# The third feed-forward group by seven products, with its token sums and its gate's weight sums on GpSimd

## The reference, cut to what matters

```
def swiglu(hn, w_ffn_in, w_ffn_out):      # hn 512 x 1024, after an RMS norm with gain
    a, b = jnp.split(hn @ w_ffn_in, 2, axis=-1)
    return (jax.nn.silu(a) * b) @ w_ffn_out        # inner width 2816
```

## Time and profile before

| | us |
|---|---|
| median of 3 runs (1831.33 to 1831.77) | 1831.52 |
| the profiled execution, its own time | 1831.15 |
| its span | 1829.3 |
| mean granted TensorE clock | 0.997 of full speed |

### The profile page before, as it was taken

How to read it: one execution, slowest core, us unless ns; L and a number is a source line. 1 busy time by engine, 2 the same in 40 slices (tenths; PEclk the granted TensorE clock), 3 DMA queues, 4 the chain that set the end, 5 groups by cost and what they waited for, 6 DMA issues and landing times.

```text
span 1829.3 us, 27260 instructions
## 1 busy us (share of the span) xinstructions
PE 1799.5 (98%) x10778; PEld 1594.2 (87%) x10778; DVE 1281.3 (70%) x1741; ACT 812.4 (44%) x1027; POOL 179.3 (10%) x97
## 2 busy tenths in 40 slices
PE   9999999999999999999999999999999999999996
PEld 8898989887888878788888999998898888999995
DVE  7566665753654737446587878887898786888786
ACT  5666666533223323224453343344545752343342
POOL 2000000010000000000001234230000001224310
PEclk9999999999999999999999999999999999999998
DMA  5012111132222221222512322322476412232331
GB/s 187 26 67 70 46 46 47 47 127 81 70 86 86 83 89 46 92 70 92 183 51 92 116 92 92 115 93 95 113 185 179 144 70 93 97 111 92 103 105 46
DMA packets 25986, 170.25 MB, mean 93 GB/s; under 512 B 2736, under 2 KB 5040, under 8 KB 6320
## 3 DMA queue, kind: packets, MB, share of 16 engines
q1 hardware_dynamic: 24176, 156.51, 24.5%
q0 software_dynamic: 1728, 12.58, 3.3%
HBM read 154.40 MB, written 2.10 MB: 86 GB/s over the span
## 4 chain that ended last, share of the span: by engine, by line
PE 90%; DVE 5%; ACT 2%; issue 2%; DMA 0%; POOL 0%; DVEq 0%; SPq 0%; ACTq 0%
PE psum L705 28%; PE psum L707 28%; PE psum L706 28%; DVE normed L1992 1%; PE psum L907 1%; PE psum L902 1%; PE psum L1049 1%; DVE h L2082 1%; ACT w_hi L1334 1%; PE psum L856 0%; ACT X_hi L1334 0%; PE psum L928 0%; PE psum L1255 0%; DMA h<-in_xfm 0%; ACT std L1334 0%
## 5 line engine op out<-in xcount | busy, mean ns | idle before, releaser
L705 PE MATMUL psum<-X_hi,w_hi 128*128 128x512 f32 (+2 forms) x1392 | 463.7, 333 | 2.8 <-issue 1.2
L707 PE MATMUL psum<-X_hi,w_lo 128*128 128x512 f32 (+2 forms) x1392 | 457.3, 329 | 0.0
L706 PE MATMUL psum<-X_lo,w_hi 128*128 128x512 f32 (+2 forms) x1392 | 457.2, 328 | 0.0
L1975 DVE TENSOR_TENSOR w_lo<-w_raw,w_hi 128x2048 fp32r<-128x2048 f32 x121 | 278.5, 2303 | 93.8 <-ACT w_hi L1334 93.4
L1334 ACT ACTIVATE w_hi<-w_raw 128x2048 fp32r<-128x2048 f32 x133 | 253.6, 1907 | 186.7 <-PE psum L707 149.6
L705 PEld LDWEIGHTS psum<-X_hi,w_hi 128*128 128x128 f32 x1392 | 262.6, 189 | 30.6 <-issue 5.9
L706 PEld LDWEIGHTS psum<-X_lo,w_hi 128*128 128x128 f32 x1392 | 263.0, 189 | 25.9 <-issue 2.4
L707 PEld LDWEIGHTS psum<-X_hi,w_lo 128*128 128x128 f32 x1392 | 262.5, 189 | 23.5
L705 PE MATMUL psum<-M_hi,w_hi 128*128 128x512 f32 x320 | 124.6, 389 | 0.0
L706 PE MATMUL psum<-M_lo,w_hi 128*128 128x512 f32 x320 | 124.6, 389 | 0.0
L707 PE MATMUL psum<-M_hi,w_lo 128*128 128x512 f32 x320 | 124.5, 389 | 0.0
(11 more groups left out here) (364 smaller groups left out, 3989.8 us busy)
## 6 DMA issues: line engine op xcount, KB each, us to landing
w_raw<-in_units SPq DMA_DIRECT2D x140, 1024.0 KB, 4.9
w_lo<-w_raw POOLq DMA_DIRECT2D x12, 1024.0 KB, 6.9
h<-in_xfm SPq DMA_DIRECT2D x4, 528.0 KB, 5.6
h<-in_xfm SPq DMA_DIRECT2D x1, 2112.0 KB, 9.3
decay<-in_dec SPq DMA_DIRECT2D x4, 512.0 KB, 5.6
out<-h SPq DMA_DIRECT2D x4, 264.0 KB, 2.3
out<-h SPq DMA_DIRECT2D x2, 496.0 KB, 2.9
rot<-in_consts SPq DMA_DIRECT2D x1, 528.0 KB, 6.9
```

Of the source, the lines that this page charges most:

```text
L705: nc.tensor.matmul(dst, w2[0], x2[0], start=first, stop=False, skip_group_check=True)
L706: nc.tensor.matmul(dst, w2[0], x2[1], start=False, stop=False, skip_group_check=True)
L707: m = nc.tensor.matmul(dst, w2[1], x2[0], start=False, stop=last, skip_group_check=True)
L1975: v.tensor_tensor(lo, w_raw[at.ring(j)][:, :], as_f32(hi), ALU.subtract).then_inc(w_lo_ready, 1)
```

## The change

`FIRST7` goes from 3 to 2: the gate and the up unit of pair 2 are made by `seven` and no more by `whole`, in each of the two blocks. `ffn1` becomes PPSEES. For that, in each block:

- The token sums go from VectorE (20 instructions of 256 columns) to GpSimd (8 of 128 x 1024: four products of an `h` quarter with the gain, four sums or differences). GpSimd starts on them at the same wait, on `post_done`, at which it filled zeros; the weight sums of pair 2's gate stand between its sixth and its seventh token sum, and the zero fill follows the eighth.
- VectorE's `wholes` begins with the splits of t1 and t2, then makes the gate of pair 1, the second weight sums of pair 2's gate, and their splits; it now waits for `acc_zero` later. ScalarE's order follows.
- The tail of `ffn1` becomes the one of a period (`downs`).
- `t_raw` lies 4 KB further on, the buffers of weight sums are ordered anew, and the two blocks use its four quarters in different orders (`t_of`).

```diff
-FIRST7 = 3
+FIRST7 = 2
-    "ffn1": (2, 3, 6, 4, 5, 0, 1, 2, 3, 6, 4, 5, 0, 3, 1, 2),
+    "ffn1": (2, 3, 6, 4, 5, 0, 1, 2, 3, 6, 4, 5, 0, 1, 3, 2, 6, 0),
-        ("ffn1", "PPPEEP"),
+        ("ffn1", "PPSEES"),
...
+    sb("t_before", [P, 2 * SEQ], F32, t_parts)
     t_raw = sb("t_raw", [P, 4, DT // 2, HT], F32, t_parts)
...
@@ GpSimd
             pool.wait_ge(post_done, (2 * n + 1) * DT)
-            nc.gpsimd.memset(acc[:, :, :], 0.0).then_inc(acc_zero, 1)
+            def quarter(name, dst, below, late):
+                rows = slice(half * below, half * (below + 1))
+                of_rows = vec[:, gain + half * below:gain + half * (below + 1)].unsqueeze(2).broadcast_to([P, half, HT])
+                nc.gpsimd.tensor_tensor(dst, h[:, rows, META + HT * late:META + HT * (late + 1)], of_rows, ALU.mult)\
+                    .then_inc(*t_sums.step(name))
+                pool.wait_ge(t_sums.sem, t_sums.at(name, n))
+            def joined(name, dst, a, b, op):
+                nc.gpsimd.tensor_tensor(dst, a, b, op).then_inc(*t_sums.step(name))
+                pool.wait_ge(t_sums.sem, t_sums.at(name, n))
...
-            first_sums(at, 4, index7(n, FIRST7, 0))
-            first_sums(at, 5, index7(n, FIRST7, 1))
+            b12, t1, t2, t4 = t_of[n]
+            quarter("b12", b12, 0, 1)
+            quarter("b11", t1, 0, 0)
+            joined("t1", t1, t1, b12, ALU.subtract)
+            quarter("b22", t2, 1, 1)
+            joined("t3", T3_raw, t2, b12, ALU.subtract)
+            joined("t2", t2, t2, t1, ALU.add)
+            pool.wait_ge(std_ready, 2 * (4 * n + 2) + 2)
+            first_sums(at, 0, index7(n, 2, 0))
+            quarter("b21", t4, 1, 0)
+            joined("t4", t4, t4, t2, ALU.subtract)
+            nc.gpsimd.memset(acc[:, :, :], 0.0).then_inc(acc_zero, 1)
+            for j, (k, c) in ((3, (2, 1)), (4, (3, 0)), (5, (3, 1))):
+                first_sums(at, j, index7(n, k, c))
@@ TensorE
-            for j in range(3):
+            for j in range(2):
                 whole(at, j, 2 * j)
-            down(at, 3, 6, base + 1)
-            whole(at, 5, 14)
+            seven(at, 2, 4, index7(n, 2, 0), True)
+            down(at, 3, 7, base + 1)
+            seven(at, 5, 15, index7(n, 2, 1))
@@ ScalarE, wholes
+                token_hi(0, "t1", 1.0)
+                token_hi(1, "t2", -1.0)
                 sigmoids(at, 0, base + 1)
+                strips(at, 1)
+                sums_hi(at, 0, index7(n, 2, 0))
+                split_hi(at, 0)
+                token_hi(2, "t4", -1.0)
                 strips(at, 3)
...
@@ VectorE, wholes
                 hidden_lo(base, *slot(0))
-                for which in ("b12", "t1", "t2", "t4"):
-                    token_sums(which)
+                token_lo(0, "t1", 1.0)
+                token_lo(1, "t2", -1.0)
                 gates_in(at, 0)
+                sums_of(at, 0, index7(n, 2, 0))
+                gates(base + 1)
+                sums_lo(at, 0, index7(n, 2, 0))
                 split_lo(at, 0)
-                gates(base + 1)
-                token_sums("t3")
-                for t, (name, scale) in enumerate((("t1", 1.0), ("t2", -1.0), ("t4", -1.0))):
-                    token_lo(t, name, scale)
+                token_lo(2, "t4", -1.0)
+                dve.wait_ge(t_high.sem, t_high.at("t3_hi", n))
+                v.tensor_tensor(late_half(X_lo), T3_raw, as_f32(late_half(X_hi)), ALU.subtract).then_inc(*t_low.step("t3_lo"))
                 ups(at, 2, base + 1)
+                chain(at, 4, index7(n, 2, 0), gate_in)
                 split_lo(at, 1)
...
+                dve.wait_ge(acc_zero, n + 1)
+                downs(at, 2, -2)
```

More of the change, by code:

```diff
@@ L361, in build @@
     t_parts = ExitStack()
+    sb("t_before", [P, 2 * SEQ], F32, t_parts)
     t_raw = sb("t_raw", [P, 4, DT // 2, HT], F32, t_parts)
     t_parts.close()
-    wx_hi = [sb(f"wx_hi{n}", [P, 3, UNIT // 4], F32R, ffns) for n in range(2)]
-    wx_lo = [sb(f"wx_lo{n}", [P, 3, UNIT // 4], F32R, ffns) for n in range(2)]
+    wx_hi, wx_lo = zip(*[[sb(f"wx_{x}{n}", [P, 3, UNIT // 4], F32R, ffns) for x in ("hi", "lo")] for n in range(2)])
+    t_of = [[t_raw[:, x, :, :] for x in order] for order in ((0, 1, 2, 3), (2, 3, 0, 1))]
     up_in = sb("up_in", [P, 2, SEQ], F32, ffns)
@@ L470, in build @@
     c7_dve = Steps(sem("c7_dve"), ["u2", "u3", "c22"])
-    t_sums = Steps(sem("t_sums"), ["b12", "t1", "t2", "t4", "t3", "t1_lo", "t2_lo", "t4_lo", "t3_lo"])
+    t_sums = Steps(sem("t_sums"), ["b12", "b11", "t1", "b22", "t3", "t2", "b21", "t4"])
+    t_low = Steps(sem("t_low"), ["t1_lo", "t2_lo", "t4_lo", "t3_lo"])
     t_high = Steps(sem("t_high"), ["t1_hi", "t2_hi", "t4_hi", "t3_hi"])
@@ L672, in _ @@
             pool.wait_ge(post_done, (2 * n + 1) * DT)
-            nc.gpsimd.memset(acc[:, :, :], 0.0).then_inc(acc_zero, 1)
+            gain = VEC["pre_ffn" + ("2" if n else "")]
+            half = DT // 2
+            def quarter(name, dst, below, late):
[7 more added lines that the diff above has]
+                pool.wait_ge(t_sums.sem, t_sums.at(name, n))
             def first_sums(at, j, idx):
@@ L1215, in period @@
             def period(at, k):
-                seven(at, 0, 0, index7(n, k, 0), True)
+                seven(at, 0, 0, index7(n, k, 0))
                 seven(at, 1, 3, index7(n, k, 1))
@@ L1757, in gated, with downs @@
                     a(silu_a[:, c, :], gate_in[:, c, :], ACT.Sigmoid).then_inc(*f_act.step(f"sig{1 - c}"))
+            def downs(at, k, s):
+                gated(k)
+                strips(at, s + 12)
+                sums_hi(at, 3, index7(n, k, 1))
+                split_hi(at, 3)
+                strips(at, s + 16)
+                sums_hi(at, 4, index7(n, k + 1, 0))
+                split_hi(at, 4)
+                takes(at, s + 17, index7(n, k, 1), up_in)
             def pair_and_gate(at, k, up_next, down_next):
@@ L1780, in period @@
                 pair_and_gate(at, k, 0, True)
[L1781 to L1788, removed]
+                downs(at, k + 1, 0)
             def final(at, k):
@@ L2564, in add_down @@
                 add_up(acc, at, s + ms[0], ms)
[L2566 to L2589, removed]
@@ L2606, in wholes @@
+                v.tensor_tensor(late_half(X_lo), T3_raw, as_f32(late_half(X_hi)), ALU.subtract).then_inc(*t_low.step("t3_lo"))
                 ups(at, 2, base + 1)
+                chain(at, 4, index7(n, 2, 0), gate_in)
                 split_lo(at, 1)
+                corner22(at, 4, index7(n, 2, 0), gate_in)
                 hidden_lo(base + 1, *slot(1))
[L2609 to L2622, removed]
+                gate_corners(at, 4, 2)
@@ L2708, in pair_and_gate, with downs @@
                 gate_corners(at, 6, k + 1)
+            def downs(at, k, s):
+                u, g = index7(n, k, 1), index7(n, k + 1, 0)
+                split_lo(at, 2)
+                gated(k)
+                add_down(at, s + 9, range(2))
+                sums_of(at, 3, u)
+                add_down(at, s + 9, range(2, 4))
+                sums_lo(at, 3, u)
+                split_lo(at, 3)
+                add_down(at, s + 9, range(4, 6))
+                sums_of(at, 4, g)
+                add_down(at, s + 9, range(6, DT))
+                sums_lo(at, 4, g)
+                chain(at, s + 17, u, up_in)
+                split_lo(at, 4)
+                corner22(at, s + 17, u, up_in)
+                sums_of(at, 5, index7(n, k + 1, 1))
+                prod(at, s + 17, k)
             def period(at, k):
-                u2, g3 = index7(n, k + 1, 1), index7(n, k + 2, 0)
                 pair_and_gate(at, k, 0, True)
[L2714 to L2731, removed]
+                downs(at, k + 1, 0)
             def final(at, k):
```

42 lines of the change are left out of this document (16 added, 26 removed).

## The result

| | before | changed |
|---|---|---|
| median, us | 1831.43 | 1849.51 (1849.16 to 1849.83) |
| ratio | 1 | 1.0098 (95% interval 1.0082 to 1.0114) |
| span of the profiled execution | 1829.3 | 1848.0 |
| mean granted clock | 0.997 | 0.993 |

A forecast was written before the change was run, and what follows sets the result against it. PE, busy 98% of the span, was taken to bound the kernel. 10.95 (first block) + 12.9 (second) - 3.2 (gain) = +20.7, giving 1852.2; with 4 us for the clock, 1856. Range 1839 to 1872.

The forecast's parts named there:

- The gain of 3.2 us: PE, gate and up in two blocks: seven products take 10.08 us against 10.88, 0.80 saved for each of four units.
- Turn-taking: GpSimd's SBUF-reading instructions and VectorE's with two SBUF inputs alternate, instruction by instruction; the forecast built on it had chance 0.62.
- steps 4 to 10: First block, in turns: from the last X_lo, ending 946.15, to the third unit's split, ending 978.15; PE stands 3.9 and 5.55 us.
- the signs given: Late X_lo, GpSimd sums before it and the adds; PE waiting 20 us and more; gates, M_lo, T_lo at two to three times.
- VectorE keeps the access: Rival: VectorE holds access over back-to-back instructions, GpSimd delays PE 1.6 us at the start; +12, 1843; chance 0.14.
- The start: First block, steps 1 to 6: turns delay the last X_lo and adds of squares; PE's sum of squares comes 5.4 us late.
- Step 1: First block: GpSimd gets its turn when X_lo of tile 6 ends, 940.56, and makes b12 to 942.86.
- GpSimd's durations: Each 128 x 1024 token sum was taken to hold the access 2.3 us (2.45 alone), bounds 2.0 to 3.4.
- my row-less term: GpSimd's token sums, with no row for 128 x 1024 or a gain spread over columns; rival of dearer sums had 0.10.
- The third unit: PE waits in ffn1 for the third unit's split by VectorE: 5.55 us in the first block, 4.8 in the second.
- the second block's first unit: Second block's ffn1: the first unit's split ends at 1494.25 behind the adds; PE stands 3.2 us for it.
- The clock: PE at half clock after five idle stretches longer than 2.7 us: between nothing and 21 us, taken as 4.

The follow-up runs named there:

- the last version: The changed kernel with token sums on VectorE, b12 and b11 on ScalarE, and GpSimd's two weight sums timed under VectorE's psum readers: 1828.51 us, ratio 0.9982.
- the pair of runs with reads and with two-input instructions beside fills: Kernel before plus six extra GpSimd sums before the zero fill: 1843.63 us; kernel before plus eight extra fills, b12 written tensor by tensor: 1831.64 us.
- The run with six reads: The kernel before with six extra GpSimd sums of two 128 x 1024 SBUF tiles ahead of the zero fill: 1843.63 us, ratio 1.0069.
- the dummies: The changed kernel with dummy matmuls in PE's idle stretches, 20 before each block's third unit, 10 before the second block's first: 1846.19 us, ratio 1.0081.
- the run with the late start: The changed kernel with GpSimd's first token sum of each block held until VectorE's last weight split before the norm's std: 1850.25 us, ratio 1.0103.

## Why the prediction was right, point by point

- **The gain of 3.2 us** held: 3.1 with fills for token sums, 3.3 in the last version (each to within about 2 us by its interval).
- **Turn-taking** held, in kind and in place: every wait that steps 4 to 10 name is in the trace (of the signs given, only the total is not: 14.2 us of new waits for "20 us and more"), and the pair of runs with reads and with two-input instructions beside fills (+12.5 and nothing) shows that it is reads against two SBUF inputs. That *VectorE keeps the access* is excluded by `X_lo` and the add of squares, each with a turn of GpSimd before it.
- **The start** was sized too high. Forecast was a sum of squares 5.4 us late, measured 946.14 - 0.48 - 943.70 = 2.0. Step 1 failed: b12 did not get its turn when the first `X_lo` ended. The add of squares behind it ran undisturbed (940.97, 0.68), and b12 came in only before the last `X_lo`, so that one turn fewer, of 2.3 us, lies ahead of the sum of squares. The two turns that are left took 1.64 and 1.70, 1.3 less than forecast together; 5.4 - 2.3 - 1.3 = 1.8. The run with six reads shows the same late first turn. Why b12 missed it no run shows.
- **GpSimd's durations.** I took 2.3 us of access for all eight. It holds for the sums (2.67 with the end of a VectorE instruction in it; 2.2 of delay in the run with reads). A product with the gain spread over its columns took 1.90 alone, and its turns some 1.7. Four such a block at 0.6 less make nearly 5 us of GpSimd's time over both blocks, not all of it shown to reach PE; this was my row-less term, and it lay outside the bounds that I gave (2.0 to 3.4).
- **The third unit** waited 4.8 and 4.0 us, for 5.55 and 4.8 forecast; the second block's first unit 2.3 for 3.2. All waits together: 14.2 us measured, and 23.9 forecast as lateness. With the dummies, where the clock never fell, the kernel is 14.8 us slower than before; the forecast without its clock term was 20.7. So the lateness, oversized by the start and by the products, holds 5.9 of the error of 6.6 us.
- **The clock** term was 4 us, and the dummies gave back 3.3 by the medians, 4.0 by the spans. The size is right, and that is partly luck: I took it from the low side of 0 to 21 and not from a row, for five long stretches. Three were followed by half clock (both waits for `X_lo` were 0.85 us and not 3.9), and one of the three slow stretches cost nothing, since PE would have waited for the third unit anyway.

## What to carry to other kernels

Before work goes to an idle GpSimd, look at what VectorE does in the same stretch: each reading GpSimd instruction that meets a VectorE instruction with two SBUF inputs costs VectorE a turn, here 1.6 to 2.2 us for 1024 columns, and if VectorE feeds the critical engine, "10% busy" is no room. Place such sums under VectorE's psum readers or its waits, and give the products that need only one tensor and a scalar to ScalarE while it idles. And a wait of PE like those here, of 2.3 to 4.8 us, is to be priced with the half clock behind it, unless PE soon waits again for an engine that is late anyway: then the slow stretch is free.

## What the runs showed of the hardware that was not expected

- A GpSimd fill held up VectorE's TENSOR_SCALAR with one SBUF input: four of 256 columns took 4.92 us for 1.14, and as TENSOR_TENSOR with the same data 1.42.
- GpSimd's product of a tensor with one value for each 256 columns takes 1.90 us for 1024 columns; a sum of two tensors about 2.4 (2.41 and 2.40 in the run with the late start).
- GpSimd's first instruction did not take the access that VectorE gave up some 0.3 us after it had started (940.72, 941.04), in both blocks of two kernels, the changed one and the one with six reads; the next ones, already waiting, did.
- After PE had stood 4.80 us it worked at half clock for 5.8 us of dense matmuls; after 4.0 us for 3.2.
